# A hybrid three-block layer on one core: the background projections' products in blocks of 24 in PE's queue

## What is computed

```python
# first block: spatial gating and gated linear attention
z = einsum('bsd,de->bse', rmsnorm(x), w_in); a_u, a_v, a_gate, b_q, b_k, b_v, b_gate, b_lr = split(z)
a_out = chunked_sgu(gelu(a_u), gelu(a_v), ...) * silu(a_gate)
o     = gla_chunked(b_q, b_k, b_v, log_a);  b_out = rmsnorm(o) * silu(b_gate)
# second block: a two-way mLSTM and attention in a window of 128 tokens
s = q k^T + bias;  prob = softmax with a sink;  out = prob v
# third block: gated DeltaNet and neighbourhood attention on a 64-wide grid
s = q k^T + rpb;   p = softmax(s, masked);      o = p v
```

## Time and profile before

| | |
|---|---|
| median of 3 runs | 3860.85 us (3857.14 to 3863.59) |
| profiled execution | 3859.77 us, span 3858.5 us, 54142 instructions |
| PE busy | 3639.6 us, 94% of the span |
| DVE, ACT, POOL busy | 2346.6, 1653.5, 751.9 us |
| mean granted clock of PE | 0.970 |
| background products L609, L610, L611 in na | 163.3, 151.0, 151.8 us busy |

### The profile page before, as it was taken

The page is one execution under the profiler, slowest core; times in us unless marked ns, Lnnn a source line. Parts: engine busy times, 40 slices in busy tenths (PEclk is TensorE's granted clock), DMA queues, the critical chain, the costliest instruction groups (busy, mean ns, idle before and its releaser), DMA issues. The chain is left out here.

```text
span 3858.5 us, 54142 instructions
## 1 busy us (share of the span) xinstructions
PE 3639.6 (94%) x20112; PEld 2867.1 (74%) x20112; DVE 2346.6 (61%) x4124; ACT 1653.5 (43%) x3090; POOL 751.9 (19%) x555
## 2 busy tenths in 40 slices
PE   8999999998998887999999989999878888999998
PEld 5787788785766775888887857767667766888886
DVE  3344332325365757877768874666666658877777
ACT  4355222314455515333334374555433325556443
POOL 1000000373002214322210150111333421000013
PEclk9999999998998999999999999999989999999999
DMA  2100111582111112465546422111121105987662
GB/s 90 33 28 28 66 43 45 193 313 90 51 43 52 59 38 99 176 207 203 184 181 233 131 53 61 47 60 46 57 82 48 53 24 191 346 310 258 206 208 97
DMA packets 219493, 456.80 MB, mean 118 GB/s; under 512 B 30544, under 2 KB 44048, under 8 KB 219240
## 3 DMA queue, kind: packets, MB, share of 16 engines
q1 hardware_dynamic: 219240, 453.45, 34.5%
HBM read 334.28 MB, written 121.05 MB: 118 GB/s over the span
## 5 line engine op out<-in xcount | busy, mean ns | idle before, releaser
L1808 PE MATMUL b_ffn_space<-b_ffn_in_hi,b_ffn_wh 128*128 128x512 f32 x1932 | 756.0, 391 | 10.7 <-DVE b_ffn_in_x_low L1301 5.2
L1810 PE MATMUL b_ffn_space<-b_ffn_in_hi,b_ffn_wl 128*128 128x512 f32 x1932 | 752.7, 390 | 0.0
L1808 PEld LDWEIGHTS b_ffn_space<-b_ffn_in_hi,b_ffn_wh 128*128 128x128 f32 x1932 | 363.2, 188 | 95.5 <-issue 12.5
L1809 PE MATMUL b_ffn_space<-b_ffn_in_x_low,b_ffn_wh 128*128 128x512 f32 x1104 | 429.6, 389 | 0.0
L1810 PEld LDWEIGHTS b_ffn_space<-b_ffn_in_hi,b_ffn_wl 128*128 128x128 f32 x1932 | 363.2, 188 | 75.8
L1809 PE MATMUL b_ffn_space<-b_ffn_in_own_low,b_ffn_wh 128*128 128x512 f32 x828 | 323.2, 390 | 0.0
L1809 PEld LDWEIGHTS b_ffn_space<-b_ffn_in_x_low,b_ffn_wh 128*128 128x128 f32 x1104 | 207.2, 188 | 42.7 <-issue 0.2
L1867 ACT ACTIVATE b_ffn_wh<-b_ffn_raw 128x512 fp32r<-128x512 f32 (+1 forms) x188 | 112.7, 611 | 210.8 <-PE b_ffn_space L1810 209.5
L1809 PEld LDWEIGHTS b_ffn_space<-b_ffn_in_own_low,b_ffn_wh 128*128 128x128 f32 x828 | 156.0, 188 | 31.9
L1699 DVE TENSOR_TENSOR b_ffn_wl<-b_ffn_raw,b_ffn_wh 128x512 fp32r<-128x512 f32 x224 | 162.7, 727 | 17.0 <-ACT b_ffn_wh L1693 16.3
L1693 ACT ACTIVATE b_ffn_wh<-b_ffn_raw 128x512 fp32r<-128x512 f32 x224 | 134.8, 622 | 83.6 <-PE b_ffn_space L1810 83.5
(11 more groups left out here) (704 smaller groups left out, 8832.9 us busy)
## 6 DMA issues: line engine op xcount, KB each, us to landing
b_ffn_raw<-w SPq DMA_DIRECT2D x96, 256.0 KB, 4.2
b_ffn_raw<-w_ffn SPq DMA_DIRECT2D x44, 512.0 KB, 4.5
b_out_block<-w SPq DMA_DIRECT2D x40, 512.0 KB, 5.6
sums_ahead<-b_out_block SPq DMA_DIRECT2D x40, 512.0 KB, 4.3
b_ffn_raw<-sums_ahead SPq DMA_DIRECT2D x80, 256.0 KB, 4.2
b3f_y<-w SPq DMA_DIRECT2D x24, 512.0 KB, 6.3
b_ffn_sums<-b3f_y SPq DMA_DIRECT2D x24, 512.0 KB, 4.6
b_ffn_raw<-b_ffn_sums SPq DMA_DIRECT2D x48, 256.0 KB, 4.5
```

The lines of the kernel that those rows point to most:

```text
L1808: self.nc.tensor.matmul(acc, self.weights.wh[w][:, wk], high[:, k], start=(k == 0), stop=False)
L1809: self.nc.tensor.matmul(acc, self.weights.wh[w][:, wk], low[:, k], start=False, stop=False)
L1810: last = self.nc.tensor.matmul(acc, self.weights.wl[w][:, wk], high[:, k], start=False, stop=(k == self.plan.rows(s) - 1))
```

## The change

The due time of a step k no longer follows k but the group of `TOGETHER` steps that it belongs to. With 8, all steps of a token half have one due time, that of the middle of the half, so nothing can be woven between them: 24 products stand in a row, still with the wait for the second piece of the weights in the middle of a first half's block.

```diff
@@ class Feed
-    PIECE = DT // 2 * P
+    PIECE, TOGETHER = DT // 2 * P, 8
@@ Feed.products
                 for k in range(DT):
-                    yield start + length * (half * DT + k) / (2 * DT)
+                    yield start + length * (half * DT + k // self.TOGETHER * self.TOGETHER + (self.TOGETHER - 1) / 2) / (2 * DT)
                     if half == 0 and k % (DT // 2) == 0:
                         pe.wait_ge(self.lo_done, 2 * b + k // (DT // 2) + 1)
```

## The result

The changed kernel takes 3972.76 us (median of four runs, 3970.84 to 3974.19) where the kernel before, run beside it, takes 3858.99: a ratio of 1.0295, 95% interval 1.028 to 1.031. The forecast was 3933, from 3882 to 3998. The direction and the range held; the cost is 114 us where the sum had 72. The profiled execution has a span of 3969.5 us, 111.0 more than before, with the same instructions.

What follows compares the result with a forecast made beforehand. PE, busy 98 to 100% in four of five stages, was taken as the bound. Stage waits of 28.3 + 19.6 + 6 + 5 + 5, clock 14, less 6 for drains, added 71.9 us: 3933 us, from 3882 to 3998.

Steps and rivals of the forecast that it cites:

- the rival of cheaper visits: Whole kernel: each visit to projection products costs PE, so 248 fewer visits give 20 us, drains 6: 3835 us; chance 0.06.
- gqa: Window attention: PE waits in gaps between blocks for transposed probabilities to be copied and for probabilities to transpose, 28.3 us.
- pairs of T and O: Transposes of probabilities (T), directly followed by the product with v (O), which waits for the copy: 18 x 0.85 us in gqa.
- The second T: In ten gqa gaps, a second transposition waits for probabilities from scores of the same gap: 1.3 us each, 13 us.
- na: Neighbourhood attention: waits for copies of transposed probabilities 11 us, between scores and transposition 5.6, norms 3; together 19.6 us.
- the norms: In na, norm sums and their spreads that now share a gap: 3 us, from 0 to 5.
- mlstm: 18 steps lose cover under DVE's busy stretches: 5 us, -1.4 to 12.4; mlstm growing most would prove the argument wrong.
- gla: Turning back normalised rows waits for their scaling in four gaps, plus 1 for states and products: +6 us, 2 to 12.
- much slower: Queues block each other, each of 67 gaps in gqa and na costs 2 us, clock falls 15 times: 4020 us; chance 0.05.
- sgu: First mixing of the second half waits 2.3 us for normalised tiles, successive mixing products 2.7: 5 us, 2 to 7.
- Clock: Long PE waits halve the granted clock: five falls in gqa, three in gla and sgu, 1.7 us each: 14 us, 0 to 26.
- Gain of the drains: In gqa and na, 38 part-array neighbours now touch without products between, saving drains: 6 us, from 4.6 to 7.6.

Runs made afterwards that it cites:

- The moved blocks: Blocks of 24 products in mlstm alone, 0.55 of a head later, single steps elsewhere, against the kernel before the change: 3866.0 us, ratio 1.0019.

## Why the prediction was right, and where its sizes were off

**The bound.** That PE has nothing in reserve held: the stages carry all of the loss, and PE's waits and clock make it up. By the batches of the Trainium skill (Perfetto Trace Analysis, Matmul Optimizations) and by the rival of cheaper visits the blocks would have gained; the measurement disagrees here, at 1.0295.

**gqa.** This term was right, in size and in mechanism. Forecast 28.3 of waits; measured 22.5 of idle and some 8 more that stand in busy time. By starts the 18 new pairs of T and O cost 18.1 us together where the forecast had 15.3: fourteen at 0.68 to 0.78 each against its 0.85, three at 1.3, and one at 3.75, where ACT's queue holds a table load and a 1.15 us activation ahead of the second copy. The idle view shows 10.1 of the 18.1. What was mis-sized lies within the pair: T and the way into O cover 0.72 us where the forecast took 0.6, and the second copy is there after 1.35 us instead of 1.45; against that, O's matmuls lose their pairing for 0.28. The second T was sized 13 and is 11.2 (13.3 less 2.1). The window's clock is 0.96. The sign "were O to find its copy ready" did not come.

**na.** Forecast 19.6; measured 21.9 of idle and some 5 more in busy time. T to O was 1.0 each in the forecast, and by starts nine undisturbed pairs took 0.87 each, of which the idle view has 0.37; one stood 2.7 us behind a late copy. S to T and the copies before T are 4.3 instead of 5.6, the norms about 11 instead of 3: this is the step that failed here. The norm's chain (sum, root, reciprocal, spread, scaling, spread) was written off in half a sentence. It holds the longest wait in the stage (3.7), and half of the falls lie behind it.

**mlstm.** Forecast 5, from -1.4 to 12.4; measured 14.4 of idle and 8.3 of clock. The failed step is the bound itself: it charged the products that lose their cover, 18 x 0.69, and took the others to cost nothing, "DVE works off its delay during blocks". DVE mostly does not: it is busy during 0.00 of 5.55 us in the block shown, and during 10.2 of the 46.9 us of all eight, because its inputs queue behind them, and works the delay off in the gap, while PE waits. The prediction named this as the sign that it would be wrong: mlstm grew most in proportion (16%; gqa 12, na 9), though not in us. The moved blocks show that it depends on place.

**gla.** Forecast 6, measured 13.6. gla_ot waits 11.1 where its pairs were sized at 9, so 7.1 more than before instead of 5. The larger miss, 5.8, is gla_o for the state: "1 for states" was mis-sized, as DVE's queue holds a split ahead of it. The rival "much slower" had this mechanism, at a size that did not come.

**sgu.** Forecast 5, measured 2.3, all of it clock. The wait for a normalised tile that the earlier trace rows led to is there, 1.5 us instead of 2.3, but other waits (sgu_acc for its low part, 5.8 to 4.2) went down by as much. The 2.7 between mixing products does not appear among PE's waits.

**Clock.** Forecast 14, measured 40 to 42. What failed is the count of the falls, and in part their length. The five stages have 31 separate stretches at half clock after the change and 12 before, 19 more where the forecast had 8. Twenty of the 31 last 3.4 us, as in the earlier trace rows, but eight last 6.8 and three, at ends of stages, 13.7 to 27.3, so that each of the 19 comes to 2.2 us and not 1.7. The count was made from gqa's gaps, with three for gla and sgu; na, given none, has 39.5 of the 85 us more at half clock, and mlstm, given none, 16.6. **This term is two thirds of the error.** Why a fall comes behind one wait and not behind another stays open.

**Gain of the drains.** Forecast -6. When idle and clock are taken off, 0.5 us are left over in gqa and -2.5 in na; with the 8 and 5 us of T and O that idle time does not hold, some -7 to -8 in each, an estimate. So more came back than the forecast took. That it is the drains was not tested: no run takes them away alone.

The sum was nearer than its terms: the clock, mlstm, gla and na's norms were too low together by more than the error, and sgu and what came back made up the rest.

## What to carry to other kernels

Independent work that is woven one step at a time between the steps of a dependent chain pays twice: it fills the chain's waits, and it keeps the other engines fed; grouped, it does the first less and can starve the others for its own length. Keep the groups short (here groups of 1.4 us of products cost 0.1%, of 2.8 us 0.9%, of 5.5 us 3%; what length of answer sets the limit was not tested), and if blocks there must be, try places where the other engines have work in hand: in mlstm that took the cost from 22 us to 6. For a forecast, price every stage's falls of the clock, not only those of the stage under study. When reading a result, compare starts: the idle view showed little more than half of what a bare pair of T and O cost.

## What the runs showed of the hardware

The clock also fell with hardly a wait before it (at 2520.12, by the record of the granted clock). PE's timeline after the change, in na, then a window of the same place:

```profile
2517.20 1.15 PE L4855 MATMUL na_norm_bank<-na_norm_rows,na_norm_spread 16*128 16x128 f32 x8
2518.50 0.77 PE L5092 MATMUL na_turned<-all_squares,na_wide 128*128 128x128 f32 x5
2519.65 1.62 PE L4855 MATMUL na_norm_bank<-na_norm_rows,na_norm_spread 16*128 16x128 f32 x8 [0.38 <-DVE na_done L4876]
...
2518.50:2521.00 2.50, 2.12 (x13) 1.88 (x13) 1.00 (x2) 1.19 (x2) 0.00 (x0) 0.82 0.00 0
```

It fell after small matmuls with one wait of 0.38 us; and after a wait of 3.59 us that ended at 299.82 (the same length as one at 269.35 behind which it did fall, at 270.73) it stayed at 1.00. So a wait's length alone doesn't tell whether a fall follows, and the same order gave different counts: na, with its order of before, had from 17.4 to 35.6 us at half clock in five kernels' profiles (17.4, 21.3, 23.0, 24.8, 35.6), and took 458.2 us in the first and 465.7 in the last.

Small DVE instructions took several times as long beside POOL. L3273 on 128x128 took 2.50 us for two at 1312.51, while POOL worked through 1309.52 to 1314.9, and 0.47 for two at 1315.38, when it had ended; of the stage's 32, the 26 without POOL beside them take 273 to 285 ns, the 6 under it 848 to 1305. Before the change it is the same (27 at 274 to 287, 5 at 883 to 1290), so it is no cost of the blocks, but in mlstm it lengthens just the chain that PE waits for.
